# Eight of twelve branch-gate projections moved to 512-column matmuls in two PSUM banks, emptied by halves

## The reference, cut to what matters

```python
proj = h @ w_in                      # the last 3 * 1024 columns are br_gate
gates = jax.nn.sigmoid(br_gate).reshape(bsz, seq, 3, D)
ys = jnp.stack([y_fox, y_sc, y_dn], axis=2)     # 3 branches, 512 channels each
merged = jnp.sum(jnp.einsum('bsnc,ncd->bsnd', ys, w_branch) * gates, axis=2)
x = x + merged @ w_o
```

## Time and profile before

| | us |
|---|---|
| median of 3 runs | 1098.03 (1098.02 to 1099.41) |
| the profiled execution | 1098.61 |
| its span in the trace | 1096.9 |
| PE, DVE, ACT busy | 1081.5, 765.2, 588.2 |
| gates 4 to 7 and branch 1 on PE, from 196.57 to | 250.81 |
| gates 11, 10, 8, 9 on PE, from 250.81 to | 278.33 |

### The profile page before, as it was taken

How to read it: one execution, slowest core, us unless ns; L and a number is a source line. 1 busy time by engine, 2 the same in 40 slices (tenths; PEclk the granted TensorE clock), 3 DMA queues, 4 the chain that set the end, 5 groups by cost and what they waited for, 6 DMA issues and landing times.

```text
span 1096.9 us, 16775 instructions
## 1 busy us (share of the span) xinstructions
PE 1081.5 (99%) x7038; PEld 949.7 (87%) x7038; DVE 765.2 (70%) x907; ACT 588.2 (54%) x731; POOL 36.9 (3%) x93
## 2 busy tenths in 40 slices
PE   9999999999999999999998999999999999999997
PEld 8899999999988888888897888888898888888886
DVE  5587888564769998886676676556578676656564
ACT  6467754336466656556655544444464766444443
POOL 6000000000000000000006000000000000000000
PEclk9999999999999999999999999999999999999999
DMA  8453433333555555555442555555544344555551
GB/s 315 158 188 116 154 128 142 117 117 123 185 183 179 190 191 192 193 192 188 172 154 85 186 192 192 192 192 192 192 134 155 135 154 167 191 188 192 189 187 58
DMA packets 27453, 185.03 MB, mean 169 GB/s; under 512 B 3169, under 2 KB 3681, under 8 KB 5618
## 3 DMA queue, kind: packets, MB, share of 16 engines
q1 hardware_dynamic: 26208, 182.46, 47.7%
q10 hardware_dynamic: 1170, 1.49, 0.4%
HBM read 182.89 MB, written 1.05 MB: 168 GB/s over the span
## 4 chain that ended last, share of the span: by engine, by line
PE 94%; DVE 3%; ACT 1%; issue 1%; DMA 0%; DVEq 0%; ACTq 0%
PE ps L2044 17%; PE ps L2114 12%; PE ps L2129 12%; PE ps L2116 12%; PE ps L2050 9%; PE ps L2082 7%; PE ps L2088 7%; PE ps L2083 7%; PE ps L2149 1%; PE ps L2064 1%; DVE low L1349 1%; PE ps L2465 1%; PE ps L2219 1%; PE ps L2317 1%; PE ps L2328 0%
## 5 line engine op out<-in xcount | busy, mean ns | idle before, releaser
L915 ACT ACTIVATE whi<-raw 128x2048 fp32r<-128x2048 f32 x170 | 324.4, 1913 | 274.9 <-PE ps L2129 132.7
L1349 DVE TENSOR_TENSOR low<-raw,whi 128x2048 fp32r<-128x2048 f32 x170 | 389.4, 2293 | 34.8 <-ACT whi L915 31.8
L2044 PE MATMUL ps<-hboth,whi 128*128 128x512 f32 x864 | 216.7, 392 | 1.2 <-DVE conv L1797 1.2
L2044 PEld LDWEIGHTS ps<-hboth,whi 128*128 128x128 f32 x864 | 157.2, 188 | 31.9 <-issue 2.5
L2114 PE MATMUL ps<-whi,ahi 128*128 128x512 f32 x416 | 163.7, 393 | 0.0
L2116 PE MATMUL ps<-whi,alo 128*128 128x512 f32 x416 | 162.7, 391 | 0.0
L2082 PE MATMUL ps<-hboth,whi 128*128 128x256 f32 x544 | 137.4, 291 | 0.0
L2083 PE MATMUL ps<-hboth,whi 128*128 128x256 f32 x544 | 133.1, 283 | 0.0
L2050 PEld LDWEIGHTS ps<-hboth,low 128*128 128x128 f32 x864 | 117.9, 190 | 8.5
L2050 PE MATMUL ps<-hboth,low 128*128 128x256 f32 x864 | 120.5, 282 | 0.0
L2129 PE MATMUL ps<-low,ahi 128*128 128x512 f32 x416 | 119.7, 389 | 0.0
(11 more groups left out here) (380 smaller groups left out, 1226.4 us busy)
## 6 DMA issues: line engine op xcount, KB each, us to landing
raw<-in_ffn_up SPq DMA_DIRECT2D x32, 1024.0 KB, 4.8
raw<-in_ffn_down SPq DMA_DIRECT2D x32, 1024.0 KB, 4.9
raw<-in_w_up SPq DMA_DIRECT2D x22, 1024.0 KB, 4.8
raw<-in_w_gate SPq DMA_DIRECT2D x12, 1024.0 KB, 4.9
raw<-in_w_down SPq DMA_DIRECT2D x11, 1024.0 KB, 4.9
raw<-in_w_dn SPq DMA_DIRECT2D x6, 1024.0 KB, 5.0
raw<-in_w_sc SPq DMA_DIRECT2D x6, 1024.0 KB, 4.8
raw<-in_w_branch SPq DMA_DIRECT2D x6, 1024.0 KB, 4.8
```

Of the source, the lines that this page charges most:

```text
L915: act.activation(whi[:, u % SPLIT, :], raw[:, u % RAW, :], ACT.Copy).then_inc(sem("hi_done"), 1)
L1349: dve.tensor_tensor(wlo[:, u % RAW, :], raw[:, u % RAW, :], whi[:, u % SPLIT, :].bitcast(F32), ALU.subtract).then_inc(sem("lo_done"), 1)
L2044: pe.matmul(out, whi[:, s, at:at + P], hboth[:, k, :, :].rearrange("p a t -> p (a t)"), start=k == 0, stop=False, skip_group_check=True)
```

## The change

Gates 4 to 11, eight of the twelve, become wide units in banks 4 and 5. Each half ends in a bank of its own with 512 columns in it. ACT copies that bank into one of the two buffers `conv` in which the convolutions worked earlier (`gate_part`, once for each half). DVE adds the left and right halves of the buffer into `gates` (`gate_part` on DVE, 128x256, once for each half). ACT takes the sigmoid of the sum in place (`gate_curve`, 128x512 in SBUF) when the unit after is through. The copy of the first half comes directly behind that half and ahead of the steps of the table; the copy of the second half is held until the next unit's first half, as the sigmoid was before. The counts of two semaphores that the feed-forward parts use are moved up by what the gates now add to them. In the diff the first `gate_part` and `gate_curve` are ACT's, the second `gate_part` and `merge` are DVE's.

```diff
     def gate(e):
-        u = unit_c(a["w_gate"][e], "h", h_ready)
+        if e < 4:
+            u = unit_c(a["w_gate"][e], "h", h_ready)
+            front.append((u, ("gate", e, u)))
+        else:
+            u = add("C", a["w_gate"][e], "h", h_ready, ["c4", "c5"], bank=4, wide=True)
+            wide_gates.append(e)
+            front.append((u, ("gate_part", e, 1, u)))
         gate_unit[e] = u
-        front.append((u, ("gate", e, u)))
...
         order.append(("mm", u, 0))
         flush()
+        if then and then[0][0] == "gate_part":
+            step("gate_part", then[0][1], 0, u)
         for s in steps_at.get(2 * at, ()):
             step(*s)
         order.append(("mm", u, 1))
+        if at and front[at - 1][1:] and front[at - 1][1][0] == "gate_part":
+            step("gate_curve", front[at - 1][1][1])
...
+            def gate_part(e, part, u):
+                n_ = wide_gates.index(e)
+                act.wait_ge(sem("unit_done") if part else sem("half_done"), u + 1)
+                if n_:
+                    act.wait_ge(sem("wide_in"), 2 * (n_ - 1) + part + 1)
+                else:
+                    act.wait_ge(sem("conv_read"), len(convs))
+                name, v = units[u]["free"][part]
+                act.activation(conv[:, part, :, PAD:PAD + T], ps[:, 4 + part, :].rearrange("p (a t) -> p a t", a=2),
+                               ACT.Copy).then_inc(sem(name), 1)
+
+            def gate_curve(e):
+                n_ = wide_gates.index(e)
+                act.wait_ge(sem("wide_in"), 2 * n_ + 2)
+                act.activation(gates[:, 2 * e:2 * e + 2, :], gates[:, 2 * e:2 * e + 2, :], ACT.Sigmoid)\
+                   .then_inc(sem("wide_part"), 1)
...
+            def gate_part(e, part, u):
+                name, v = units[u]["free"][part]
+                dve.wait_ge(sem(name), v + 1)
+                dve.tensor_tensor(gates[:, 2 * e + part, :], conv[:, part, 0, PAD:PAD + T], conv[:, part, 1, PAD:PAD + T],
+                                  ALU.add).then_inc(sem("wide_in"), 1)
...
             def merge(n_, g, b, u):
...
-                dve.wait_ge(*took(gate_unit[4 * n_ + 2 * g + b]))
+                e = 4 * n_ + 2 * g + b
+                if e in wide_gates:
+                    dve.wait_ge(sem("wide_part"), wide_gates.index(e) + 1)
+                else:
+                    dve.wait_ge(*took(gate_unit[e]))
```

More of the change, by code:

```diff
@@ L248, in z @@
         front.append((u, ("z", e, u)))
-    gate_unit = {}
+    gate_unit, wide_gates = {}, []
     def gate(e):
-        u = unit_c(a["w_gate"][e], "h", h_ready)
+        if e < 4:
[5 more added lines that the diff above has]
+            front.append((u, ("gate_part", e, 1, u)))
         gate_unit[e] = u
-        front.append((u, ("gate", e, u)))
     fox(0, 0)
@@ L1122, in up_first @@
                     act.wait_ge(sem("glu_lo") if part else sem("glu_prod"), c)
-                act.wait_ge(sem("wide_in"), n_ + 1)
+                act.wait_ge(sem("wide_in"), 2 * len(wide_gates) + n_ + 1)
                 for q in range(2):
@@ L1199, in relu2_split @@
             def relu2_split(i, c, down):
-                act.wait_ge(sem("wide_in"), 2 * NF + i + 1)
+                act.wait_ge(sem("wide_in"), 2 * len(wide_gates) + 2 * NF + i + 1)
                 if down is not None:
@@ L1307, in _ @@
                          fox_cum=fox_cum, att_scores=att_scores, att_turn=att_turn, fox_out=fox_out, z=z,
-                         gate=gate,  dn_decay=dn_decay, dn_x0=dn_x0, dn_y=dn_y,
+                         gate=gate, gate_part=gate_part, gate_curve=gate_curve, dn_decay=dn_decay, dn_x0=dn_x0, dn_y=dn_y,
                          dn_off=dn_off, dn_sol=dn_sol, dn_out=dn_out, merge=merge, ple_gate=ple_gate, ple_p=ple_p,
@@ L1793, in up @@
                 n_ = 2 * c + part
-                dve.wait_ge(sem("wide_part"), n_ + 1)
+                dve.wait_ge(sem("wide_part"), len(wide_gates) + n_ + 1)
                 both = ps[:, units[u]["bank"]:units[u]["bank"] + 2, :].rearrange("p c (a t) -> p c a t", a=2)
@@ L1797, in up @@
                 own(dve.tensor_tensor(here, both[:, :, 0, :], upart[part], ALU.add), *took_name(u))
-                own(dve.tensor_tensor(here, here, wide(rwide[:, :].unsqueeze(1), [2, T]), ALU.mult), "wide_in", n_ + 1)
+                own(dve.tensor_tensor(here, here, wide(rwide[:, :].unsqueeze(1), [2, T]), ALU.mult), "wide_in", 2 * len(wide_gates) + n_ + 1)
             def up_taps(c, part):
@@ L1869, in relu2 @@
             def relu2(i, u):
-                dve.wait_ge(sem("wide_part"), 2 * NF + i + 1)
+                dve.wait_ge(sem("wide_part"), len(wide_gates) + 2 * NF + i + 1)
                 y = cy[:, i % 2, :, :]
@@ L1874, in relu2 @@
                 own(dve.scalar_tensor_tensor(out=y, in0=y, scalar=0.0, in1=y, op0=ALU.max, op1=ALU.mult),
-                    "wide_in", 2 * NF + i + 1)
+                    "wide_in", 2 * len(wide_gates) + 2 * NF + i + 1)
             def relu2_split(i, c, down):
@@ L1968, in _ @@
             gla_qk_ready = [took(s[2]) for s in order if s[0] == "gla_qk"][2:]
-            parts = dict(norm=norm, norm_first=norm_first, norm_sum=norm_sum, norm_wide=norm_wide, ab_qk=ab_qk,
+            parts = dict(norm=norm, norm_first=norm_first, norm_sum=norm_sum, gate_part=gate_part, norm_wide=norm_wide, ab_qk=ab_qk,
                          pool_u=pool_u, gla_key=gla_key, gla_qk=gla_qk,
```

## The result

| | before | after |
|---|---|---|
| median of the runs, us | 1098.72 (1098.02 to 1100.93, 4 runs) | 1107.41 (1105.36 to 1108.8, 4 runs) |
| profiled execution, us | 1098.61 | 1107.75 |
| its span, us | 1096.9 | 1106.0 |
| gate 4's first matmul to w_o's first, us | 196.57 to 289.85 = 93.28 | 198.83 to 298.90 = 100.07 |

The ratio is 1.0077 [1.0064, 1.0089]: the changed kernel is 0.8% slower. 1104.8 was forecast, in a range of 1101.3 to 1108.2. "The stretch" is from here on what the last line of the table spans. PE's own order of work in it is fixed, so what PE loses there is read from it without anything that happens at the start or the end of the program. It grew by 6.79 us, and 6.73 was forecast.

The account below looks back on a forecast made before the run. PE was taken to bound the kernel, busy 99% of the span; waits of 4.77 + 0.86 + 2.38 = 8.01 us less 1.28 saved gave 6.73 us more, 1104.8 us on the median, range 1101.3 to 1108.2.

Parts of the forecast that it names:

- waits of the first kind: Behind first halves of gates 4, 5, 6: PE's dn_y waits for masked copies queued behind DVE's addition; 3 x 1.59 us.
- The second kind: Branch unit behind gate 5: second half's addition delays DVE's masked copies and weight split; PE waits 0.54 + 0.32 us.
- The third kind: ACT between gates 10 and 8: sigmoid and table loads delay the copy freeing bank 5; PE waits 2.38 us.
- The rival by which the squares run early: At gate 10, ACT reaches the squares of dn_sum early and the third kind hides; 1102.4 us, chance 0.08.
- the drain at table loads: Both table switches at gate 10 drain as long again as a load, 2.6 us more, 1107.4 us; chance 0.05.
- the wait that moves on: Margins at gate 9 and the branch unit are used up by 1 to 3 us on ACT; 1106 to 1108, chance 0.09.
- Gate 9 and the branch unit behind it: Gate 9's second half finds its bank 0.5 us early, the branch unit dn_lo 0.7 us early; neither waits.
- PE's saving: Wide halves of gates 4 to 11 take 2.80 us instead of 2.88, 0.08 saved on each of 16: 1.28 us.
- The sum: Whole stretch: waits of 4.77 + 0.86 + 2.38 = 8.01 us, less 1.28 saved, 6.73 us more.

Follow-up runs that it names:

- the later additions: Changed kernel with DVE's additions as a step of their own behind the second half's weight split, ACT's copies unmoved; 1102.59 us, ratio 1.0037 to the kernel before.
- the early four: Kernel before with only gates 4 to 7 made wide, gates 8 to 11 as before; 1103.5 us, ratio 1.0045.
- the version without waits: All eight gates wide, rearranged; behind gate 5 DVE takes masked copy, then gate 5's last addition, then gate 4's merge; 1098.0 us, ratio 0.9996 to the kernel before.
- the late four: Kernel before with only gates 8 to 11 made wide, gates 4 to 7 as before; 1101.11 us, ratio 1.0027.
- the repeated run: The changed kernel again with no edit, timed against the kernel before; 1107.09 us, ratio 1.0074.
- the late sigmoid: Changed kernel with only gate 11's sigmoid moved behind the first half of gate 8; 1103.68 us, ratio 1.0042 to the kernel before.
- both together: Changed kernel with DVE's additions behind the steps and gate 11's sigmoid one unit later; 1104.38 us, ratio 1.0046 to the kernel before.
- the second version: All eight gates wide, rearranged, gate 4's merge back in its place, gate 5's last addition and sigmoid behind the masked copies; 1098.91 us, ratio 1.0002 to the kernel before.

## Why the prediction was right

**The waits of the first kind** were forecast at 3 x 1.59 and came at 1.61, 1.55 and 1.62, at the three `dn_y` named. What they are was shown by the later additions, which took all three away, and by the early four wide alone, which have them unchanged.

**The second kind**, forecast 0.54 + 0.32, was read as 0.54 and 0.32. The early four alone have both, and with the additions behind the split the first of them is gone.

**The third kind**, forecast 2.38, was 2.25, for the reason given: the sigmoid later by half a unit took the wait away. The rival by which the squares run early did not come; they ran at 272.83, behind the sigmoid of 272.30. Nor did the drain at table loads, which would have made it 1107.4 with the other waits. That this is the measured median is chance, as it is that the median lies in the band of the wait that moves on. The loads of 271.00 and 273.98 take 1.28 each, the next instruction follows 0.02 or less behind them, and ahead of the first there is no pause (270.39 + 0.60 = 270.99). The Trainium skill, ScalarE: Activation LUTs, section "What ACT_TABLE_LOAD costs", adds a drain to each; this trace does not have one.

**Gate 9 and the branch unit behind it** were said not to wait, with 0.5 and 0.7 us to spare, and do not. In the trace of after ACT has emptied gate 9's second bank at 284.03, 0.56 ahead of PE's start at 284.59, and DVE has finished `dn_lo` at 286.63, 0.75 ahead of 287.38.

**PE's saving** is the term that was mis-sized: 1.28 forecast, 1.10 in the trace of after, 0.99 in the version without waits. The forecast multiplied one reading, that of a half behind another half, by 16. Here are the first rows of such groups of before, of a half behind 128-wide matmuls and one behind a half:

```profile
260.12 0.36 PE L2082 MATMUL ps<-hboth,whi 128*128 128x256 f32 x1
...
263.07 0.28 PE L2082 MATMUL ps<-hboth,whi 128*128 128x256 f32 x1
```

The first group lasts 2.00 (to 262.12), the second 1.93 (to 265.00). In the trace of after the half behind another half has 270.19 to 272.03, 1.84: 0.09 saved. But the half at gate 4 (198.83 to 200.79) has 1.96 against 2.00 (196.57 to 198.57): 0.04 saved. Of the 16 halves most stand behind small matmuls, and over all 16 it is 0.06 to 0.07 each. The Trainium skill, TensorE: Matmul & The Clock Gate, section "Wait — 56ns, not 53.3ns?", puts a fixed 2.5 ns on each warm matmul. An estimate from it for the 128 matmuls left out is 0.32; the measured 1.0 to 1.1 is three times as much, so for these matmuls the row was the better guide, though not one row for all.

**The sum** was right for the stretch (6.73 forecast, 6.79 read) and for the lowest runs (1104.74 against 1097.88, 6.86). It was short for the median, which is 8.7 above before's. The forecast's sum held the granted clock at 1.00 throughout and named no rival for the clock. The runs showed that PE's standing still is sometimes followed by a time at the lower level: 3.09 us in one trace of the changed kernel, some 1.6 in that of the late four. That the median of 1107.41 still lies inside the range is luck in this respect, for the room came from other terms, larger waits in the three places, which did not come. With the same waits filled, the median came down by 2 us. In the first trace of after the stretch has none of it, and its surplus over the forecast lies at the start: 6.79 + 2.26 = 9.05 of the 9.1 us by which the span grew.

## What to carry to other kernels

An addition of 0.4 us on an engine with 30% to spare cost 1.6 us, three times, since it waited for the newest result and the oldest need stood behind it in the queue. For each inserted instruction, ask when its inputs are ready and what the bound engine takes from behind it; put it behind that. The wide form's own gain here (1.0 us) is so small that a single misplaced instruction outweighs it, and of six rearranged versions four still waited, three of them at a place where the changed kernel had not, which only following each queue to the next instruction of PE shows.

A gap on PE can cost more than its length: compare lowest runs as well as medians, and read the granted clock behind each gap.

## What the runs showed of the hardware

Behind a wait of PE the granted clock fell in some executions and not in others of the same program. In the stretch it did so behind one of the twelve waits of 1.6 us that the traces of after, the repeated run, the late sigmoid and the early four have. It did so behind four of the five longer ones (2.25 to 3.6 us, at gate 8 or 9) in the traces of after, the repeated run, the later additions, both together and the late four. Each such fall cost much the same, 1.5 to 1.6 us. A shorter pair of waits, 1.38 and 0.79 us near 590, was followed by one in 8 of 14 traces, for 0.8 to 1.2 us. At the start of the program one followed 1.90 us in which PE stood still, in the trace of after (1.64 us lost), and none followed 1.49 us in that of the second version. With matmuls that compute nothing in the place of the waits the clock in the stretch was 1.00 in the one trace taken, and the five runs lay within 0.94 us of each other, where ten runs of the changed kernel spread over 4.06. What decides in which execution it falls was not found.

The time that a group of matmuls takes depends on what went before it. In the trace of after the same eight 512-column matmuls took, from their first start to the next group's, 1.84 us directly behind the 256-column ones of another half, 1.92 to 1.93 behind 128-column and 1.94 to 1.96 behind 64-column ones.
